# A relative bias table: 128 stored copies read with a row step of 511, in place of overlapping rows and a flip matmul

## What is computed

```
rel = k_pos[None, :] - (start + jnp.arange(Q_BLOCK))[:, None]
bias = rel_table[rel_bucket(rel)].astype(jnp.float32)
logits = logits + bias.transpose(2, 0, 1)[None, :, None]
p = jax.nn.softmax(logits, axis=-1)
```

## Time and profile before

| | us |
|---|---|
| median of 3 runs | 2584.17 (2583.9 to 2584.44) |
| span of the profiled execution, first to last instruction | 2582.4 |
| TensorE busy | 2531.2 (98%) |
| VectorE busy | 1424.9 (55%) |
| ScalarE busy | 532.5 (21%) |
| GpSimd busy | 319.5 (12%) |

### The profile page before, as it was taken

The page is one execution under the profiler, slowest core; times in us unless marked ns, Lnnn a source line. Parts: engine busy times, 40 slices in busy tenths (PEclk is TensorE's granted clock), DMA queues, the critical chain, the costliest instruction groups (busy, mean ns, idle before and its releaser), DMA issues. The chain is left out here.

```text
span 2582.4 us, 38687 instructions
## 1 busy us (share of the span) xinstructions
PE 2531.2 (98%) x16224; PEld 1968.4 (76%) x16224; DVE 1424.9 (55%) x2632; ACT 532.5 (21%) x1249; POOL 319.5 (12%) x367
## 2 busy tenths in 40 slices
PE   8999999999999999999999999999999999999998
PEld 7888886864688898687458757888887656656997
DVE  1575454865247544482345825555433478963775
ACT  1342220100035121111012921000002243321000
POOL 2001111210100121031000000000000145510110
PEclk9999999999999999999999999999999999999999
DMA  7341114986543211488652012222221534434553
GB/s 265 114 121 61 45 57 147 300 292 239 178 123 114 83 35 51 139 281 294 239 186 82 18 33 82 88 92 74 90 98 43 162 115 127 131 97 151 168 172 106
DMA packets 253604, 341.82 MB, mean 132 GB/s; under 512 B 7252, under 2 KB 179412, under 8 KB 253304
## 3 DMA queue, kind: packets, MB, share of 16 engines
q1 hardware_dynamic: 241632, 311.71, 37.1%
q10 hardware_dynamic: 8920, 17.67, 2.1%
q0 software_dynamic: 2880, 9.96, 1.0%
HBM read 338.13 MB, written 1.19 MB: 131 GB/s over the span
## 5 line engine op out<-in xcount | busy, mean ns | idle before, releaser
L1001 PE MATMUL PS<-MEM 128*128 128x256 f32 (+1 forms) x2632 | 447.9, 332 | 2.6 <-ACT MEM L1458 1.2
L1001 PEld LDWEIGHTS PS<-MEM 128*128 128x128 f32 x2632 | 406.3, 190 | 43.8 <-issue 1.9
L398 PE MATMUL PS<-MEM 128*128 128x256 f32 x1632 | 356.2, 379 | 0.3 <-DMA MEM<-w_up 0.3
L1417 ACT ACTIVATE MEM<-PS 128x256 f32<-128x256 f32 (+4 forms) x405 | 167.3, 429 | 900.7 <-PE PS L398 221.7
L398 PEld LDWEIGHTS PS<-MEM 128*128 128x128 f32 x1632 | 308.5, 190 | 43.2 <-issue 1.3
L444 PE MATMUL PS<-MEM 128*128 128x512 f32 x608 | 265.6, 597 | 10.5 <-DMA MEM<-w_down 6.1
L2025 DVE SCALAR_TENSOR_TENSOR MEM<-MEM 128x512 f32<-128x512 f32 x280 | 216.0, 804 | 65.1 <-DMA MEM<-ada_w 59.2
L444 PEld LDWEIGHTS PS<-MEM 128*128 128x128 f32 x608 | 115.2, 191 | 157.1 <-issue 140.9
L2913 POOL TENSOR_TENSOR MEM<-MEM 128x1 f32<-128x1 f32 (+1 forms) x34 | 21.6, 634 | 1269.0 <-DVE MEM L1971 810.3
L670 PE MATMUL PS<-MEM 128*128 128x256 f32 x768 | 172.3, 382 | 0.0
L1314 PE MATMUL PS<-MEM 128*128 128x512 f32 (+1 forms) x512 | 170.2, 485 | 0.0
(11 more groups left out here) (383 smaller groups left out, 3267.7 us busy)
## 6 DMA issues: line engine op xcount, KB each, us to landing
MEM<-w_in SPq DMA_DIRECT2D x54, 1024.0 KB, 5.5
MEM<-ada_w SPq DMA_DIRECT2D x48, 1024.0 KB, 7.5
MEM<-w_up SPq DMA_DIRECT2D x32, 1024.0 KB, 5.5
MEM<-w_down SPq DMA_DIRECT2D x32, 1024.0 KB, 5.2
MEM<-ssm_w_in SPq DMA_DIRECT2D x24, 1024.0 KB, 5.4
MEM<-ffn_gate SPq DMA_DIRECT2D x22, 1024.0 KB, 5.3
MEM<-ffn_up SPq DMA_DIRECT2D x22, 1024.0 KB, 5.3
MEM<-ffn_down SPq DMA_DIRECT2D x20, 1024.0 KB, 5.1
```

The costliest lines, as they stand in the source:

```text
L398: ins = pe.matmul(bank[:, 0:T], W[:, k, c * P:(c + 1) * P], XT[:, k, :], start=k == 0, stop=k == KT - 1)
L1001: ins = pe.matmul(out, left[:, k, :], right[:, k, :], start=k == 0, stop=k == 3)
L1417: act.activation(out, view(b), func, **kw).then_inc(S("bank_read_by_act"), 1)
```

## The change

The ACT engine stores each of the 4 vectors 128 times: `bias_dram` grows from 4 x 512 to 4 x 128 x 512 values, 1 MB. The 8 loads of POOL read with a step of 511 values between rows: row p lies in copy p and starts one place earlier in it than row p - 1 did in its own. So the rows come in the right order and go straight to `BIAS`. The flipped identity, its load, the 4 matmuls and the 4 copies are gone. DVE waits for the 8 loads ahead of its copies of the mixing, and ACT waits for the store where it waited for `bias_done`.

```diff
@@ tiles @@
-        FLIP = mem(P, at=part + 512)
-        BRAW = mem(NH1, NT, T, at=part + 2048)
@@ TensorE @@
-            def relative_bias():
-                pe.wait_ge(S("bias_raw"), 16 * NH1 * NT)
-                for h in range(NH1):
-                    bank = take(("bias", h), "dve")
-                    done(pe.matmul(bank, FLIP, BRAW[:, h, :, :].rearrange("p a b -> p (a b)"), start=True, stop=True))
...
-            pe.wait_ge(S("bias_loaded"), 48)
+            pe.wait_ge(S("bias_loaded"), 32)
...
                 if l == 0:
-                    relative_bias()
                     pe.wait_ge(S("tables_loaded"), 16)
@@ ScalarE @@
-            act.dma_start(FLIP[:, :], io["flip"]).then_inc(S("bias_loaded"), 16)
...
-                        act.dma_start(io["bias_dram"], BV[0:NH1, 0:512]).then_inc(S("bias_stored"), 16)
+                        act.dma_start(io["bias_dram"], BV[0:NH1, 0:512].unsqueeze(1).to_broadcast([NH1, P, 512])).then_inc(S("bias_stored"), 16)
...
-                    act.wait_ge(S("bias_done"), 1)
+                    act.wait_ge(S("bias_stored"), 16)
@@ VectorE @@
                 if l == 0:
-                    for h in range(NH1):
-                        b = filled(dve, "dve", ("bias", h))
-                        read(dve.tensor_copy(BIAS[:, h, :, :].rearrange("p a b -> p (a b)"), b))
-                    settle()
-                    dve.nop().then_inc(S("bias_done"), 1)
+                    dve.wait_ge(S("bias_raw"), 16 * NH1 * NT)
@@ GpSimd @@
-                    src = bass.AP(tensor=io["bias_dram"].tensor, offset=512 * h + 128 - P * q, ap=[[1, P], [1, T]])
-                    pool.dma_start(BRAW[:, h, q, :], src).then_inc(S("bias_raw"), 16)
+                    src = bass.AP(tensor=io["bias_dram"].tensor, offset=512 * P * h + 255 - P * q, ap=[[511, P], [1, T]])
+                    pool.dma_start(BIAS[:, h, q, :], src).then_inc(S("bias_raw"), 16)
@@ host @@
-    io["bias_dram"] = nc.dram_tensor("bias_dram", (NH1, 512), F32, kind="Internal").ap()
+    io["bias_dram"] = nc.dram_tensor("bias_dram", (NH1, P, 512), F32, kind="Internal").ap()
```

More of the change, by code:

```diff
@@ L3146 @@
         "x": a["x"], "w_in": a["w_in"], "w_branch": a["w_branch"], "w_out": a["w_out"], "w_up": a["w_up"], "w_down": a["w_down"],
-        "cst": constants(), "onehot": bucket_onehot(), "flip": np.eye(P, dtype=np.float32)[::-1].copy(),
+        "cst": constants(), "onehot": bucket_onehot(),
         "pv": pv, "rel_bias": a["rel_bias"], "da_lambda": a["da_lambda"], "ln_rows": np.array(rows),
```

## The result

| | before | changed |
|---|---|---|
| median, us | 2584.17 (4 runs, 2583.9 to 2584.44) | 2607.59 (4 runs, 2606.76 to 2608.39) |
| span of the profiled execution, us | 2582.4 | 2605.4 |
| mean granted TensorE clock | 0.999 | 0.994 |

The ratio is 1.0091, 95% interval 1.0078 to 1.0103: slower by 0.9%, where 0.14% faster was forecast. The time lies far outside the range of 2579.8 to 2585.0.

A forecast was written before the change was run, and what follows sets the result against it. TensorE was taken as the bound, everything else merely having to be in time. Span 2582.4 - 3.44 (matmuls) - 0.19 (`flip`) + 0 = 2578.8 us; with the median 1.77 above the span, 2580.5 us, range 2579.8 to 2585.0.

The forecast's parts named there:

- The store's time: 1 MB store on ACT's queue, issued at 13 us: forecast to take 6 or 24 us, landing near 19 or 37.
- Both ends: Store's possible spreads: sixteen DMA engines with 64 KB each, 6 us, or four with 256 KB each, 24 us.
- both spreads: Store on sixteen or on four DMA engines: no stall forecast under either, and 2580.5 us both times.
- Rival 2: ACT can't issue `da_lambda` and the tables until the store is through; TensorE stalls 14.9 us, 2595.4; chance 0.08.
- 152 rows: Store, `da_lambda` and tables on ACT's queue, set against some 190 rows under way when SP was let go.
- Rival 1: A slab comes late on the full DMA engines: stall up to 4.9 us, middle 2, 2582.5, at most 2585.4; chance 0.14.
- While ACT's queue is backed up, SP keeps its share: Slabs on SP's queue: slab 3 lands at 32 to 35 and slab 4 at 37 to 43, in time.
- The added 248 KB an engine: Extra traffic on four DMA engines that competes with slabs 2 to 5; no stall was taken for it.
- the removed matmuls' 3.44 us: Four matmuls in eight passes, from 72.12 to 75.56 on TensorE's line: 3.44 us saved, carried to the end.
- the bias copies: VectorE's four copies, 0.69 us each: said to cost nothing before and so to give nothing when removed.
- `da_lambda`, the tables and POOL's loads: Transfers behind the store: all forecast late but hidden, the loads by 20 us, ACT's delay with 19 us to spare.
- The -0.19 for `flip`: Dropped 64 KB load ahead of slab 1's end, for which TensorE waited: 0.19 us saved at 348 GB/s.

The follow-up runs named there:

- With ScalarE free to issue: The changed kernel with `da_lambda` and the tables issued ahead of the 1 MB store in ACT's queue: 2603.98 us, ratio 1.0075.
- the wide store: The changed kernel with the vectors written to all 128 partitions and the store reading each partition four times, on 16 engines: 2581.45 us, ratio 0.9990.

## Why the prediction was wrong

- **The store's time**, the step that failed. "At ACT's share the store takes 64 / 10.6 = 6 us or 256 / 10.6 = 24 us": it took 46, from 12.6 to 58.9. Both ends came from rows of loads, spread over all partitions. A store that reads four neighbouring partitions 128 times each has no row before, and it moved 23 GB/s over its whole time and 25 when it was alone. The two ends had assumed 4 x 10.6 = 42 and 16 x 10.6 = 170 GB/s beside the other queues. The number of engines was taken as the unknown, and that was the wrong unknown. The four engines were right. That the sum came out the same under both spreads was no safety: with the store on sixteen engines the time is 2610.6, as bad.
- **What bounds it.** The Trainium skill ("SBUF — State Buffer", section "Door 1: The DMA port swizzle (why `[64,N]` ≈ `[32,N]`)") says that DMA reaches the partitions through 16 ports of 27.2 GB/s, that partitions 0 to 3 and 32 to 35 have one of them and 64 to 67 and 96 to 99 another, and that partitions 8 apart below 32 have different ones. From its figure, one, two and four ports would give 27, 54 and 109 GB/s, an estimate. The measured 25 to 27 GB/s agree, and so do the 50 for two ports (0, 32, 64, 96), the 100 for four (0, 8, 16, 24), and the order of the landings at 59, 39 and 34. The 33 GB/s from partitions 0 to 3 between 18 and 22 us, and the 67 from 0, 32, 64, 96 between 24.0 and 25.5, lie above one and two times 27.2; there the trace doesn't agree, and no run tells why. The runs show that the source's place is the cause; that it is this port is the page's account of it.
- **Rival 2, ACT held at its queue** (0.08), is what happened, at the place and nearly at the price named: 14.9 us forecast, 13.12 measured. The argument against it failed. It compared 152 rows (144 by the changed kernel's trace, where the tables come as 128 rows, 8 an engine) with an estimate of 190 taken from SP's slabs, which drain fast; here `da_lambda` was held for 18.46 us. "Full rings" is the prediction's reading; the runs show the hold and not what is full.
- **Rival 1, a late slab** (0.14), happened as well, at slab 4, and 8.18 us exceed its bound of 4.9, which rested on the same rate. "While ACT's queue is backed up, SP keeps its share" failed too: from 24 to 30 us SP's queue moved 0.07 MB, 12 GB/s, one row for each row of the slow store, and from 55 to 58 nothing. With ScalarE free to issue, TensorE waited 5.34 us for slab 3 and 11.62 for slab 4. (The added 248 KB an engine should be 254, which changes nothing.) The two were priced as alternatives, though both follow from one slow store and add up.
- **The clock** was in no rival. A long wait costs more than its length: 2.95 and 2.3 us of passes at the lower level came on top.
- **Right**: the removed matmuls' 3.44 us lie on TensorE's line (with the wide store the mixing comes 3.50 earlier: 3.44, and 0.16 of an earlier start, less 0.09 of slower first passes); the bias copies were free (VectorE sat idle for 17.77 us before the mixing's first copy); `da_lambda`, the tables and POOL's loads, late as they were, cost nothing that shows here, with TensorE itself 24 us late: the first mixing copy was still released by TensorE. The -0.19 for `flip` came out as 0.09 here, and as 0.04 to 0.25 in the other kernels without its load.

## What to carry to other kernels

Before a broadcast by DMA is put in place of a matmul, ask from how many partitions it reads, not only how many bytes it moves or how many engines it gets: 1 MB out of four neighbouring partitions took 46 us, out of all 128 it took 13, on full engines. Such a transfer hurts others more than itself. Look at what stands behind it in its queue, at the engine that has to issue it, and at the slabs that share the DMA engines; a high DMA share next to few GB/s is its mark.

## What the runs showed of the hardware

- Reading from partitions 0 to 3 gave 25 to 27 GB/s in all when little else moved, on 4 or on 16 engines, into DRAM or into SBUF; from 0, 32, 64, 96 it gave 50, from 0, 8, 16, 24 it gave 100. Beside full traffic (18 to 22 us) all three gave 33.
- A transfer can keep all 16 engines busy at 38 GB/s in total, and slabs of another queue then crawl with it: TensorE waited 30.3 us.
- An engine that issues behind a backed-up queue stands still, 18.46 us here for an issue that takes 0.35.
- TensorE stood idle from about 24.6 us; the granted clock was 1.00 until 28, 0.97 from 28 to 30 and 0.50 from 30 on. From 38 to 42, with work again, it was still 0.50, then 0.81 from 42 to 46 and 1.00 from 46.
